# Hybrid decoder layer, the hand-over from the mixer to the MLP: two raw weight tiles fetched one by one and sooner, the first Relu pair ahead of six squares, the third mixing sum moved between the MLP's first matmuls

## The reference, cut to what matters

```python
merged = sum_i sigmoid(gate_i) * (branch_i @ w_proj_i)     # three branches
x  = x + rms_norm(merged @ w_out, norm_post_mix)           # "mixing" norm
h2 = rms_norm(x, norm_pre_mlp)                             # "pre" norm
ff = square(relu(h2 @ mlp_w1)) @ mlp_w2                    # 1024 -> 4096 -> 1024
x  = x + rms_norm(ff, norm_post_mlp)
```

## Time and profile before

| what | value |
|---|---|
| median of three runs | 2102.9 us |
| the profiled execution's own time | 2102.35 us |
| its span | 2100.7 us |
| PE busy | 2007.6 us (96%) |
| DVE, ACT, POOL busy | 959.9, 541.4, 665.5 us |
| mean granted TensorE clock | 0.984 of full |

### The profile page before, as it was taken

One profiled execution on the slowest core, in us unless ns is written; L12 is line 12 of the kernel. 1 busy time (PEld: TensorE's weight loads), 2 busy tenths in 40 slices (PEclk: granted clock), 3 DMA queues, 4 the chain that ended last, 5 costly groups with the idle time before them and its releaser, 6 DMA issues.

```text
span 2100.7 us, 32964 instructions
## 1 busy us (share of the span) xinstructions
PE 2007.6 (96%) x13822; PEld 1907.1 (91%) x13822; DVE 959.9 (46%) x1320; ACT 541.4 (26%) x815; POOL 665.5 (32%) x352
## 2 busy tenths in 40 slices
PE   4999999999999999998999998799999999999997
PEld 4999899998999986778999998799999999999996
DVE  7894441245544426663355836752223222222227
ACT  4212211243334326674100134220101010010102
POOL 1222111111111113343466611124343434343453
PEclk8999999999999999999999999799999999999998
DMA  3333436466667533212344333201111111111132
GB/s 133 96 95 104 110 102 187 145 212 201 211 200 225 187 130 117 82 48 82 124 170 139 130 96 102 89 21 48 44 48 44 41 51 41 51 41 51 41 133 83
DMA packets 151478, 223.50 MB, mean 106 GB/s; under 512 B 34576, under 2 KB 108560, under 8 KB 151344
## 3 DMA queue, kind: packets, MB, share of 16 engines
q1 hardware_dynamic: 139248, 193.42, 30.0%
q10 hardware_dynamic: 12096, 28.12, 3.7%
HBM read 173.84 MB, written 45.56 MB: 104 GB/s over the span
## 4 chain that ended last, share of the span: by engine, by line
PE 89%; DVE 6%; ACT 2%; issue 1%; DMA 1%; POOL 0%; SPq 0%; POOLq 0%; DVEq 0%; ACTq 0%
PE ps L1815 69%; PE ps L2011 3%; PE ps L2111 2%; PE ps L2038 2%; PE ps L2050 2%; PE ps L2203 2%; PE ps L1835 1%; PE ps L1954 1%; PE ps L1916 1%; PE ps L1935 1%; PE ps L2180 1%; DMA w_raw<-in_w 1%; PE ps L1903 1%; PE ps L1943 0%; PE ps L1899 0%
## 5 line engine op out<-in xcount | busy, mean ns | idle before, releaser
L747 POOL TENSOR_TENSOR w_hi<-w_raw,zeros 128x1024 fp32r<-128x1024 f32 x78 | 189.2, 2426 | 543.4 <-PE ps L1815 476.6
L1815 PE MATMUL ps<-op_hi,w_hi 128*128 128x352 f32 x1536 | 344.7, 333 | 9.0 <-DVE op_lo L1542 5.1
L739 POOL TENSOR_TENSOR w_lo<-w_raw,w_hi 128x1024 fp32r<-128x1024 f32 x54 | 133.0, 2464 | 653.2 <-ACT w_hi L840 653.2
L1815 PE MATMUL ps<-op_lo,w_hi 128*128 128x352 f32 x1536 | 334.2, 326 | 0.0
L1815 PE MATMUL ps<-op_hi,w_lo 128*128 128x352 f32 x1536 | 332.2, 324 | 0.0
L1815 PEld LDWEIGHTS ps<-op_hi,w_hi 128*128 128x128 f32 x1536 | 259.8, 189 | 20.8 <-issue 14.2
L1815 PEld LDWEIGHTS ps<-op_lo,w_hi 128*128 128x128 f32 x1536 | 263.1, 189 | 0.0
L1815 PEld LDWEIGHTS ps<-op_hi,w_lo 128*128 128x128 f32 x1536 | 262.2, 189 | 0.0
L749 POOL TENSOR_TENSOR w_lo<-w_raw,w_hi 128x1024 fp32r<-128x1024 f32 x78 | 203.5, 2609 | 6.1
L1815 PE MATMUL ps<-hid_hi,w_hi 128*128 128x352 f32 x816 | 177.1, 325 | 4.2 <-DVEq L1705 2.3
L1815 PE MATMUL ps<-hid_lo,w_hi 128*128 128x352 f32 x816 | 177.7, 326 | 0.0
(11 more groups left out here) (301 smaller groups left out, 3055.7 us busy)
## 6 DMA issues: line engine op xcount, KB each, us to landing
w_raw<-in_w SPq DMA_DIRECT2D x148, 512.0 KB, 3.7
kc<-in_k_cache SPq DMA_DIRECT2D x48, 448.0 KB, 5.1
vc<-in_v_cache SPq DMA_DIRECT2D x48, 448.0 KB, 6.5
out_keep<-stage ACTq DMA_DIRECT2D x24, 528.0 KB, 2.7
tmp_gate_d<-stage ACTq DMA_DIRECT2D x24, 528.0 KB, 4.4
gate_t<-tmp_gate_d SPq DMA_DIRECT2D x24, 528.0 KB, 3.7
qkv<-out_keep SPq DMA_DIRECT2D x15, 512.0 KB, 4.9
acc<-in_x SPq DMA_DIRECT2D x8, 528.0 KB, 6.8
```

The source lines that it names most:

```text
L739: pool.tensor_tensor(w_lo[:, b].rearrange("p k m -> p (k m)"), w_raw[:, b], w_hi[:, b].rearrange("p k m -> p (k m)").bitcast(F32), ALU.sub ...
L747: pool.tensor_tensor(hi.rearrange("p (a m) -> p a m", a=2), w_raw[:, b].rearrange("p (a m) -> p a m", a=2), zeros[:].unsqueeze(1).broadcas ...
L1815: mm = pe.matmul(ps[:, 3 * dst + q, 0:BLK], w[:, b, w0 + n], x[:, k, q * BLK:(q + 1) * BLK], start=(n == 0 and part == 0), stop=(n == len( ...
```

## The change

It moves three things and removes or adds no arithmetic.

1. SP: the pair fetch `weights(P_MLP + 1)` behind `x2_row(1, 3)` is gone. Tile 2 is fetched behind `x2_row(1, 0)` and tile 3 behind `x2_row(1, 2)`, each by `weight_tile`.
2. ACT: of the eight squares of the third piece two stay ahead of `first_relu(0)` and `first_relu(1)`, and six (k = 2 to 7) go behind them.
3. PE: `mix_total(2)` stood behind the 24 matmuls of tile 0, piece 0; it now stands behind the first 12 of them (k = 0 to 3).

```diff
@@ SyncE, the loop over q and k
-                    if q == 1 and k == 3:
-                        weights(P_MLP + 1)
+                    if q == 1 and k in (0, 2):
+                        weight_tile(2 * (P_MLP + 1) + k // 2)
@@ ScalarE, after mlp_high(2, k)
-            for k in range(KD):
+            for k in range(2):
                 pre_square(2, k)
@@ ScalarE
             for b in range(2):
                 first_relu(b)
+            for k in range(2, KD):
+                pre_square(2, k)
             pre_root(2)
@@ TensorE, inside the loops over q and b
                     for k in range(KD):
                         first_up(b, k, q)
-                    if (q, b) == (0, 0):
-                        mix_total(2)
+                        if (q, b, k) == (0, 0, 3):
+                            mix_total(2)
```

## The result

The changed kernel took 2090.4 us (median of four runs, 2088.61 to 2090.90) against 2102.9 us for the kernel before (four runs, 2102.39 to 2103.46): the ratio is 0.9935, with a 95% interval of 0.9923 to 0.9947. The forecast was 2088.9 us in a range of 2086.0 to 2092.4. The profiled execution took 2088.61 us and spans 2087.0 us; the sum of the prediction, made against the profiled execution, gave 2088.3.

A forecast was written before the change was run, and what follows sets the result against it. PE bounds the kernel, so time is won only where it stands still or runs at its lower clock. 3.28 - 1.94 + 10.5 + 2.2 = 14.0 us off the 2102.9 us median gives 2088.9 us, range 2086.0 to 2092.4.

The forecast's parts named there:

- Part 1: Earlier fetch on SP: ACT reaches raw tile 2 without waiting, so the mixing total comes 3.28 us sooner.
- Part 2: Mixing total on PE behind 12 matmuls instead of 24: 12 matmuls shift behind the wait before it, costing 1.94 us.
- Part 3: Six squares behind the Relu pair on ACT: Relu starts with tile 0's end, MLP tile 2 gains 10.5 us from the order.
- The clock: PE's MLP tile 2, after a wait of only 0.8 us, runs at the higher clock; 2.2 us come back.
- The adds: Six moved squares' adds on DVE beside POOL's split end by 1349.8 to 1350.4, before the 1350.65 need; no cost taken.
- A: Rival: the early fetch buys nothing, the mixing total stays at 1316.04; gain 10.8 us, time 2092.1 us; 12 in 100.
- B: Rival: the six adds bound the total behind tile 2, 1 to 5 us late; 2090 to 2096 us; 12 in 100.
- C: Rival: the clock helps behind hole 3, or the loss behind hole 1 is smaller; 2086.0 to 2087.4 us; 12 in 100.
- hole 1: PE's wait before the third mixing total, 9.85 us before the change, forecast about 8.5 us.
- D: Rival: slower than before, the clock does not come back behind hole 1; 2108 us and above; 2 in 100.
- E: Rival: no change, something other than the Relu held MLP tile 2; 2 in 100.
- hole 3: PE's wait before the general loop, 2.26 us, forecast to stay as it is.

The follow-up runs named there:

- quiet_12: Changed kernel with POOL's split of tiles 4 and 5 waiting for the last add; median 2089.3 us, ratio 0.9928 to the kernel before.
- back_quiet: Changed kernel with the mixing total back behind 24 matmuls and POOL's split waiting for the last add; median 2085.0 us, ratio 0.9915 to the kernel before.
- back_quiet_again: back_quiet run once more, unchanged; median 2087.25 us, ratio 0.9918 to the kernel before.
- total_back: Changed kernel with the mixing total put back behind 24 matmuls; median 2089.1 us, ratio 0.9928 to the kernel before.
- total_only: Kernel before with only the mixing total moved, behind 12 matmuls instead of 24; ratio 0.9996 to the kernel before.
- split_later: Kernel before with POOL's split of tiles 4 and 5 waiting until all third-piece squares are added; median 2097.2 us, ratio 0.9970.
- relu_only: Kernel before with only the six squares moved behind the Relu pair; median 2092.9 us, ratio 0.9947 to the kernel before.
- fetch_only: Kernel before with only the earlier fetch of tiles 2 and 3; median 2100.9 us, ratio 0.9983 to the kernel before.
- same_again: Changed kernel run once more, unchanged; profiled execution 2089.47 us, ratio 0.9932 to the kernel before.

## Why the prediction was right, point by point

- **Part 1, 3.28 us.** Measured 3.30 at the mixing total (1312.74 for 1316.04), and 3.29 alone. ACT came to the raw tile at 1297.55 (1297.54 said) and found it there. That the adds' blocking beside POOL's low parts would move along unchanged held: the next row of DVE's chain is 2.12 us (2.13 before).
- **Part 2, 1.94 us lost.** Measured as 1.95 between quiet_12 and back_quiet, and 2.39 against back_quiet_again. So parts 1 and 3 made the gain and part 2 gave some of it back: 0.97 us as the adds stand (total_back), about 2 us once they are out of the way. total_only shows the condition the sum rests on: the loss is there only once the squares no longer hold the Relu.
- **Part 3, 10.5 us.** The Relu started at 1337.64 (1337.6 said), tile 2 at 1338.88 (1338.8). Alone it gave 10.75. split_later divides it: 5.8 us of POOL's blocking, 4.7 of the squares themselves.
- **The clock, 2.2 us.** Tile 2 took 1350.57 - 1338.88 = 11.69 us instead of 13.98, which is 2.29; 11.80 was said. A hole of 0.80 us left the clock at 1.00. The other half of the premise, that a hole of 2.26 us brings the lower clock, held in seven of 13 profiles only; the term did not rest on it, since tile 2 had 11.26 us of idle time ahead of it before and 0.80 after.
- **The adds, no cost.** Said to end at 1349.8 to 1350.4 before a need at 1350.65; they ended at 1350.11 before 1350.57. relu_only and total_back, where POOL's split lies later against the Relu, show what happens without the cover: 1.16 and 0.97 us. The near end, 1349.8, comes out of no sum shown there: one blocked add fewer would be 2.58 - 0.63 = 1.95 us better, 1348.4.
- **Rivals.** A falls with fetch_only. B has the right mechanism and a size that four passes limit. C did not occur in the profiled execution and is real all the same, as luck of one execution: the first 1152 matmuls of the general loop take 187.14 us in six of the 13 profiles and 188.66 or 188.67 in seven, 1.5 us apart where the prediction had between 0.5 and 2.2, and the loss behind hole 1 is up to 0.9 us smaller in some. D and E did not occur. E's argument read the wrong row: 1309.87 is the end of tile 3's high part, that of tile 2 was done at 1300.82 + 1.06 = 1301.88, which makes the argument stronger.
- **From the profile to the median.** This step was off: the profiled execution hit the sum to 0.3 us, but the median lies 1.8 us above it, where I had carried over the 0.55 us of the kernel before. The 13 profiles show three sources of spread: where the stretch starts (4.7 us from end to end, with PE's wait for `hid_lo` and the clock behind the waits there), the clock behind hole 1 (up to 0.9 at holes of one length) and behind hole 3 (1.5). The profiled execution was one of the early ones in the first. That the unprofiled runs differ by the same three is argued from this, not shown.

That the Trainium skill's exclusive port (SBUF — State Buffer, "SBUF: two separate sides") blocks an add until the pass ends agrees with the four adds of relu_only, 2.09 and three times 2.55 us beside 0.54. These traces show besides that one waiting add got in behind each of POOL's passes: four passes blocked three or four adds and never more.

## What to carry to other kernels

When a stage ends in one engine's queue, ask which of the instructions ahead of the releasing one need not be there: here six squares, tied to another engine's adds, held an instruction that needed nothing from them, and moving them was worth over three times as much as the earlier fetch. Put work behind a wait only if it is needed later than the wait ends: 12 matmuls moved from in front of a hole to behind it cost their full time, but this shows only after the next hole has gone, so judge each part of a change with the others in place. Keep a stream of short dependent adds on DVE away from two-input work on POOL, and when several us of noise lie ahead of the stretch, compare profiles from a common event.

## What the runs showed of the hardware

- An add on DVE that waits beside POOL's passes ends some 0.4 us after a pass has ended (1345.42 against 1345.02 in relu_only), and POOL's next pass is longer by it: 2.69 and 2.56 us where adds slipped in, against 2.38 to 2.40 where POOL was alone (the changed kernel's rows above and those of split_later).
- TensorE's clock stayed up behind every hole of 0.80 us looked at. Behind hole 3, always 2.2 to 2.3 us, it fell to 0.50 in seven of 13 profiles and stayed at 1.00 in six, so the length of a hole of this size does not tell which. Ahead of the stretch it fell behind a wait of 2.18 us in the first profile of the changed kernel, and in same_again stayed up behind 2.11 and fell behind 2.44. Behind the same hole of 8.50 us what was lost differed by 0.86 us between executions (59.73 and 58.87 us to the Relu).
- Two executions of the same program can agree to 0.01 us over 87 us and differ by 1 us ahead of it.
